# Convolution in VectorE's gaps between score levels, three modulation tiles summed in its place, out projection ahead of the ones products

## What is computed

```python
# modulation, for both layers: 24 tiles of 512 columns (tiles 0 to 11 layer 0, 12 to 23 layer 1)
mod[l] = silu(c) @ mod_w[l] + mod_b[l]            # 1024 -> 6 * 1024
# layer 0
q, f_raw, i_val, g_out, z, xbc, dt_raw = split(h @ w_in)
o_a = hgrn2_chunk_scan(q, 1 - f, i_val, log(f))    # gated recurrence, 8 heads of 128
o_a = group_rms_norm(o_a, hg_norm, 8) * silu(g_out)
xbc = silu(causal_dwconv(xbc, conv_w, conv_b))     # 4 taps, 1536 channels = 12 blocks of 128
xs, bm, cm = split(xbc)
y = ssd_chunk_scan(xs, dt, a, bm, cm) + d_skip * xs    # 16 heads of 64
o_b = group_rms_norm(y * silu(z), ssm_norm, 2)     # two groups of 512
x = x + gate * (concat(o_a, o_b) @ w_out)          # 2048 -> 1024
```

## Time and profile before

| | us |
|---|---|
| three executions | 1159.43, 1163.57, 1165.64 (median 1163.57) |
| profiled execution | 1162.93 |
| its span, first to last instruction | 1161.2 |
| PE busy | 1105.4 (95% of the span) |
| DVE busy | 428.9 (37%) |
| ACT busy | 266.7 (23%) |
| mean granted clock of TensorE | 0.974 of full |

### The profile page before, as it was taken

One profiled execution on the slowest core, in us unless ns is written; L12 is line 12 of the kernel. 1 busy time (PEld: TensorE's weight loads), 2 busy tenths in 40 slices (PEclk: granted clock), 3 DMA queues, 4 the chain that ended last, 5 costly groups with the idle time before them and its releaser, 6 DMA issues.

```text
span 1161.2 us, 15296 instructions
## 1 busy us (share of the span) xinstructions
PE 1105.4 (95%) x6223; PEld 719.1 (62%) x6223; DVE 428.9 (37%) x951; ACT 266.7 (23%) x439; POOL 107.4 (9%) x138
## 2 busy tenths in 40 slices
PE   4899999998989999999999989999998999999997
PEld 2686688896358864444444568848887844444444
DVE  0353674247460131222111386874523411111213
ACT  2212111223340131111111255323321311111113
POOL 5012112020000010000000201311000100000000
PEclk9899899999989989999999999999988999999998
DMA  9797747247978459997999920100059599999992
GB/s 350 267 371 290 263 172 279 84 145 259 390 293 342 164 197 422 421 421 287 421 420 420 344 104 21 53 0 3 2 199 420 210 401 420 421 420 420 421 421 85
DMA packets 86452, 320.55 MB, mean 276 GB/s; under 512 B 9877, under 2 KB 11253, under 8 KB 61813
## 3 DMA queue, kind: packets, MB, share of 16 engines
q1 hardware_dynamic: 83144, 309.49, 68.2%
q0 software_dynamic: 2448, 8.91, 2.0%
q10 hardware_dynamic: 796, 1.23, 0.3%
HBM read 316.47 MB, written 3.15 MB: 275 GB/s over the span
## 4 chain that ended last, share of the span: by engine, by line
PE 83%; SPq 6%; DMA 4%; DVE 3%; ACT 2%; issue 1%; ACTq 1%; DVEq 0%
PE bank L1178 17%; PE bank L811 17%; PE bank L1211 9%; PE bank L872 7%; PE bank L1103 6%; PE bank L822 5%; SPq L585 3%; PE bank L938 2%; DMA arena<-in_moe_w 2%; PE bank L844 1%; PE bank L1186 1%; PE bank L781 1%; PE bank L1475 1%; SPq L513 1%; PE bank L1465 1%
## 5 line engine op out<-in xcount | busy, mean ns | idle before, releaser
L811 PE MATMUL bank<-arena,ring 128*128 128x256 f32 x960 | 212.9, 383 | 3.9 <-ACT arena L1648 2.7
L811 PEld LDWEIGHTS bank<-arena,ring 128*128 128x128 f32 x960 | 183.3, 192 | 30.2 <-issue 3.9
L1178 PE MATMUL bank<-ring,arena 128*64 128x512 f32 x704 | 153.7, 592 | 0.0
L1178 PEld LDWEIGHTS bank<-ring,arena 128*64 128x64 f32 x704 | 50.4, 137 | 99.4 <-issue 99.4
L2386 DVE TENSOR_TENSOR arena<-arena,bank 128x512 f32<-128x512 f32 x17 | 18.1, 1068 | 224.5 <-PE bank L1178 224.5
L872 PE MATMUL bank<-arena,ring 128*128 128x256 f32 x384 | 86.0, 388 | 2.8 <-issue 2.8
L1178 PE MATMUL bank<-arena 128*64 128x512 f32 x384 | 84.4, 593 | 2.1 <-DMA arena<-in_moe_w 2.1
L1103 PE MATMUL bank<-arena 128*128 128x256 f32 x336 | 84.3, 398 | 2.0 <-DVE arena L2404 2.0
L872 PEld LDWEIGHTS bank<-arena,ring 128*128 128x128 f32 x384 | 74.8, 195 | 13.9 <-issue 3.2
L1103 PEld LDWEIGHTS bank<-arena 128*128 128x128 f32 x336 | 63.6, 199 | 11.5 <-issue 3.7
L1211 PE MATMUL bank<-ring,arena 128*64 128x512 f32 x288 | 63.8, 595 | 0.0
(11 more groups left out here) (373 smaller groups left out, 1360.6 us busy)
## 6 DMA issues: line engine op xcount, KB each, us to landing
ring<-in_moe_w SPq DMA_DIRECT2D x112, 1024.0 KB, 16.0
arena<-in_moe_w SPq DMA_DIRECT2D x80, 1024.0 KB, 19.0
ring<-in_mod_w SPq DMA_DIRECT2D x24, 2048.0 KB, 11.3
ring<-in_ev_w_in SPq DMA_DIRECT2D x13, 2048.0 KB, 12.8
ring<-in_od_w_rkv SPq DMA_DIRECT2D x6, 2048.0 KB, 13.3
ring<-in_ev_w_out SPq DMA_DIRECT2D x4, 2048.0 KB, 17.3
ring<-in_od_w_o SPq DMA_DIRECT2D x2, 2048.0 KB, 10.2
token_rows<-arena SPq DMA_DIRECT2D x2, 1024.0 KB
```

Source lines behind the costliest of these rows:

```text
L811: mm = pe.matmul(ps[:, c * S:(c + 1) * S], w_cols(slot)[:, k, (2 * half + c) * P:(2 * half + c + 1) * P], src[:, k, :], start=(k == 0), st ...
L1178: mm = pe.matmul(bank[4 + half][e * C:(e + 1) * C, :], hgT[:, kb, e * C:(e + 1) * C], piece(slots[e], kb), start=(kb == 0), stop=(kb == KB ...
```

## The change

Five edits, all in layer 0.

- `conv(b)` becomes a function, called in DVE's loop over the score levels: blocks 0 to 5 after `level_mult(5)`, 6 to 9 after `level_diff(7)` and the step of dt, 10 and 11 after `level_mult(7)`. ACT's silu of the convolution moves ahead of the evacuation of g_out.
- Modulation tiles 12, 13 and 14 are summed by DVE (`mod_sum`) where the convolution stood, into `buf(7)`; three products of ones (`ones_slide`, made by POOL) put them into strips 0, 1 and 2 of the row bank. Their slots come free by `mod_summed`.
- The modulation steps between the pairs of HGRN2 outputs are gone; the first one left, tile 15, follows the sum of squares. The transposes wait for `o_evac` one by one.
- `gate_scan` puts line 2206 and line 2243 together into DVE's decay loop at h = 3.
- The modulation columns move into PE's decay loop at h = 14 and their taking on DVE to h = 16; the out projection's first tile goes ahead of the ones products of y, which come before the second tile.

```diff
@@ -62,6 +62,7 @@
 MOD_DVE = 12
+MOD_LATE = 15
 NSUB = 4
@@ -359,7 +360,12 @@
             return [g for g, (a, b) in enumerate(MOD_GROUPS) if a <= m < b][0]
-        mod_acc = [buf(10)[:, i * W:(i + 1) * W] for i in (0, 1, 3, 2)]
+        ones_slide = buf(1)[:, 3 * W:3 * W + 63]
+        mod_acc_early = [buf(10)[:, i * W:(i + 1) * W] for i in (0, 1, 3, 2)]
+        mod_acc_late = [buf(7)[:, i * W:(i + 1) * W] for i in range(MOD_LATE - MOD_DVE)]
...
+        def mod_acc(m):
+            return mod_acc_early[m % 4] if m < MOD_DVE else mod_acc_late[m - MOD_DVE]
         def mod_slot(m):
@@ -529,7 +535,7 @@
                 at = places[l, kind].index(n)
-                if kind == "mod" and MOD_FIRST <= 12 * l_mod + j < MOD_DVE:
+                if kind == "mod" and MOD_FIRST <= 12 * l_mod + j < MOD_LATE:
                     sp.wait_ge(mod_summed, 12 * l_mod + j + 1 - MOD_FIRST)
@@ -711,7 +717,8 @@
             pool.wait_ge(proj_full, FULL_IN)
-            link(pool.memset(slide[1], 0.0))
+            link(pool.memset(buf(1)[:, 2 * W:3 * W + 63], 0.0))
+            pool.memset(ones_slide[:, 31:32], 1.0)
             pool.tensor_copy(slide[1][:, :, 31], csilu[:]).then_inc(basics, 1)
@@ -842,23 +849,21 @@
                         mm = pe.matmul(row_bank[32 * c:32 * (c + 1), :], slide[g][:, k, 31 - i:63 - i],
-                                       w_cols(slot)[:, k, :], start=(m == a and r == 0), stop=(m == b - 1 and r == 1),
+                                       w_cols(slot)[:, k, :], start=(r == 0 and (m == 0 or m == MOD_LATE and c == 3)), stop=(m == b - 1 and r == 1),
                                        skip_group_check=True)
...
                 for q in range(4):
-                    mm = pe.matmul(bank[6][:, 4 * m + q:4 * m + q + 1], mod_acc[m % 4][:, q * P:(q + 1) * P],
+                    mm = pe.matmul(bank[6][:, 4 * m + q:4 * m + q + 1], mod_acc(m)[:, q * P:(q + 1) * P],
                                    ones[:, 0:1], start=True, stop=True)
                 mm.then_inc(mod_full, 1)
-            mod_next = [MOD_DVE]
+            mod_next = [MOD_LATE]
             def modulation_step():
                 if mod_next[0] < 24:
-                    if mod_next[0] == 12:
-                        pe.wait_ge(basics, 3)
                     modulation(mod_next[0], bank[0])
@@ -983,7 +988,6 @@
                 mm.then_inc(o_full, 1)
-                modulation_step()
             pe.wait_ge(dt_ready, 1)
@@ -994,9 +998,10 @@
             pe.wait_ge(conv_silu, 1)
-            pe.wait_ge(o_evac, 4)
             for u in range(4):
                 tt, half = u // 2, u % 2
+                if u in (1, 2):
+                    pe.wait_ge(o_evac, u + 2)
                 if u == 3:
@@ -1004,6 +1009,13 @@
+            pe.wait_ge(basics, 3)
+            pe.wait_ge(mod_summed, MOD_LATE - MOD_FIRST)
+            for i in range(MOD_LATE - MOD_DVE):
+                mm = pe.matmul(bank[0][32 * i:32 * (i + 1), :], ones_slide[:, 31 - i:63 - i], mod_acc(MOD_DVE + i),
+                               start=True, stop=False, skip_group_check=True)
+            mm.then_inc(mod_full, MOD_LATE - MOD_DVE)
             pe.wait_ge(xdt_ready, 3)
@@ -1024,6 +1036,7 @@
                 mm.then_inc(stat_full, 1)
+            modulation_step()
             pe.wait_ge(cb_ready, 2)
@@ -1051,18 +1064,26 @@
                     head_out(h - 3)
-            mod_columns(1, bank[2])
...
-            pe.wait_ge(squares_ready, 1)
-            pe.wait_ge(dec_diff, NH)
-            for g in range(GROUPS):
-                for k in range(4):
-                    mm = pe.matmul(bank[4][:, g * S:(g + 1) * S], ones[:, 0:P], fT[:, 4 * g + k, :],
-                                   start=(k == 0), stop=(k == 3))
-            mm.then_inc(stat_full, 1)
-            pe.wait_ge(mod_taken, 3)
-            out_projection(0, places[0, "out"][0], 4, lambda i: oa[:, i, :] if i < KB else yT[:, i - KB, :],
-                           lambda j: pe.wait_ge(oa_ready, 1) if j == 0 else pe.wait_ge(ob_ready, 1))
+                if h == NH - 2:
+                    mod_columns(1, bank[2])
...
+            def out_ready(j):
...
+                if j == 0:
+                    pe.wait_ge(mod_taken, 3)
+                    pe.wait_ge(oa_ready, 1)
+                elif j == 1:
+                    pe.wait_ge(squares_ready, 1)
+                    pe.wait_ge(dec_diff, NH)
+                    for g in range(GROUPS):
+                        for k in range(4):
+                            mm = pe.matmul(bank[4][:, g * S:(g + 1) * S], ones[:, 0:P], fT[:, 4 * g + k, :],
+                                           start=(k == 0), stop=(k == 3))
+                    mm.then_inc(stat_full, 1)
+                else:
+                    pe.wait_ge(ob_ready, 1)
...
+            out_projection(0, places[0, "out"][0], 4, lambda i: oa[:, i, :] if i < KB else yT[:, i - KB, :], out_ready)
             def moe(l, k):
@@ -1738,6 +1759,8 @@
             level_exp(7)
+            act.wait_ge(conv_done, XBLK)
+            act.activation(xpad[:, :, TAPS - 1:], xpad[:, :, TAPS - 1:], ACT.Silu).then_inc(conv_silu, 1)
             act.wait_ge(mod_full, MOD_DVE)
@@ -1747,8 +1770,6 @@
                 act.activation(dst(fT), bank[6 + u % 2][:], ACT.Square).then_inc(o_evac, 1)
-            act.wait_ge(conv_done, XBLK)
-            act.activation(xpad[:, :, TAPS - 1:], xpad[:, :, TAPS - 1:], ACT.Silu).then_inc(conv_silu, 1)
             for u in range(4):
@@ -2015,9 +2036,10 @@
                 slot, count = mod_slot(m)
-                acc = mod_acc[m % 4]
+                acc = mod_acc(m)
                 dve.wait_ge(tile_landed[slot], 16 * count)
-                dve.wait_ge(mod_full, max(MOD_FIRST, m - 3))
+                if m < MOD_DVE:
+                    dve.wait_ge(mod_full, max(MOD_FIRST, m - 3))
                 link(ts_(acc, w_cols(slot)[:, 0, :], csilu[:, 0:1], None, ALU.mult))
@@ -2127,6 +2149,16 @@
                     ins.then_inc(score_evac, 1)
+            def conv(b):
...
+                dve.wait_ge(proj_evac, 18)
+                tmp = ctmp[:, b % 2, :]
+                wt = lambda j: col("ev_conv_w", j * XBLK + b)
+                link(ts_(tmp, xpad[:, b, 0:S], wt(0), col("ev_conv_b", b), ALU.mult, ALU.add))
+                for j in range(1, TAPS - 1):
+                    link(stt(tmp, xpad[:, b, j:j + S], wt(j), tmp, ALU.mult, ALU.add))
+                stt(xpad[:, b, TAPS - 1:], xpad[:, b, TAPS - 1:], wt(TAPS - 1), tmp, ALU.mult,
+                    ALU.add).then_inc(conv_done, 1)
             level_diff(0)
@@ -2143,6 +2175,12 @@
                     mod_sum(m)
+                if i == 5:
+                    for b in range(6):
+                        conv(b)
+                elif i == 7:
+                    for b in range(10, XBLK):
+                        conv(b)
                 if i < 7:
@@ -2152,6 +2190,8 @@
                     ts_(dts[:, 0, :], bank[7][0:NH, 0:S], dt_bias[:], None, ALU.add).then_inc(dtz, 1)
+                    for b in range(6, 10):
+                        conv(b)
                 if i == 6:
@@ -2171,15 +2211,8 @@
             gains(0, 1)
-            dve.wait_ge(proj_evac, 18)
-            for b in range(XBLK):
-                tmp = ctmp[:, b % 2, :]
-                wt = lambda j: col("ev_conv_w", j * XBLK + b)
-                link(ts_(tmp, xpad[:, b, 0:S], wt(0), col("ev_conv_b", b), ALU.mult, ALU.add))
-                for j in range(1, TAPS - 1):
-                    link(stt(tmp, xpad[:, b, j:j + S], wt(j), tmp, ALU.mult, ALU.add))
-                stt(xpad[:, b, TAPS - 1:], xpad[:, b, TAPS - 1:], wt(TAPS - 1), tmp, ALU.mult,
-                    ALU.add).then_inc(conv_done, 1)
+            for m in range(MOD_DVE, MOD_LATE):
+                mod_sum(m)
             dve.wait_ge(dtN_full, 1)
@@ -2200,15 +2233,18 @@
             dve.wait_ge(proj_evac, 26)
-            for u in range(4):
-                dve.wait_ge(stat_rstd, u + 1)
-                for h in (2 * u, 2 * u + 1):
-                    ins = stt(oa[:, h, :], oa[:, h, :], col("ev_hg_norm", h), fT[:, h, :], ALU.mult, ALU.mult)
-            count[0] += 1
-            ins.then_inc(dve_chain, 1)
-            normed = count[0]
...
...
+            def gate_scan():
...
+                for u in range(4):
+                    dve.wait_ge(stat_rstd, u + 1)
+                    for h in (2 * u, 2 * u + 1):
+                        ins = stt(oa[:, h, :], oa[:, h, :], col("ev_hg_norm", h), fT[:, h, :], ALU.mult, ALU.mult)
+                link(ins)
+                tt_(buf(2), buf(2), buf(10), ALU.mult).then_inc(oa_ready, 1)
...
...
+            dve.wait_ge(mod_full, MOD_LATE)
             def decay_diff(h):
@@ -2237,15 +2273,14 @@
                     decay_mult(h - 1)
-                if h == NH + 1:
...
-                    dve.wait_ge(dve_chain, normed)
-                    tt_(buf(2), buf(2), buf(10), ALU.mult).then_inc(oa_ready, 1)
+                if h == 3:
+                    gate_scan()
```

(5 more changed lines are left out.)

## The result

The changed kernel takes 1151.88 us, the median of five executions (1150.28 to 1155.23), against 1163.57 before: a ratio of 0.989, with 0.9865 to 0.9914 as its 95% interval. 1151.0 was forecast.

A forecast was written before the change was run, and what follows sets the result against it. PE, busy 95%, was taken as the bound, then DVE and the modulation loads. Out projection 15.6 us earlier less 3.8 for ones products gives 11.8, called 12: 1162.9 - 12 = 1151.0 us, range 1146 to 1157.

The forecast's parts named there:

- The convolution at no cost: Score levels: twelve blocks of 1.89 us fit DVE's idle gaps, the tight two with 1.0 and 0.8 us to spare.
- Three tiles summed by DVE: Ahead of the decay loop: PE sheds three 1.85 us steps, pays 0.9; first decay row moves from 293.99 to about 286.3.
- Tile 23 stops it: Decay loop: tile 23 cannot land before 310.8, so PE waits and only 5.2 of 8.6 us come through.
- The rate: Modulation loads after tile 17: 5.47 us per 2.10 MB tile, 384 GB/s, queue never empty from 269 on.
- Tail and out projection: End of decay loop: out projection begins at 328.5 instead of 344.14, 15.6 us earlier, paying back 3.8 for ones products.
- its first tile (a quarter of 55.42, 13.9 us): Out projection: the first tile takes 13.9 us and covers the last y, ACT's squares and their wait.
- The sum: Layer 0's mixer: 15.6 - 3.8 = 11.8 us gained, called 12 us and counted whole to the kernel's end.
- the second rival: PE's clock drops at waits for transfers and thin work until 328, costing 2.0 to 5 us: about 1154.5; chance 0.2.
- Rivals 3 and 4: Layer 0's experts' transfers absorb most gain, about 1161, chance 0.05; convolution overruns its gaps, about 1165, chance 0.04.
- the fourth rival: Score levels: blocks at 2.0 times their length overrun DVE's gaps, PE waits 14 us; about 1165, chance 0.04.

The follow-up runs named there:

- e9: Kernel before with only the convolution moved into DVE's gaps, ACT's silu ahead and transposes waiting one by one; median 1163.72 us, 0.999 of before.
- e10: Changed kernel plus four PE products nobody reads, in the wait before the first score level; median 1151.43 us, 0.9894 of before.
- e4: Changed kernel with modulation tiles 18 and 19 issued ahead of tile 17 on SP's queue; median 1147.8 us, 0.9842 of before.
- e5: Changed kernel plus six PE products nobody reads, three before the wait for tile 22, three before head 14; median 1152.62 us, 0.9887 of before.
- e1: Kernel before with only convolution in the gaps, three tiles summed by DVE, first modulation step after the sum of squares; median 1159.38 us, 0.9957 of before.
- e3: Changed kernel with the ones products of y back ahead of the out projection's first tile; median 1158.34 us, 0.9943 of before.
- e7: Changed kernel with ten convolution blocks instead of six in DVE's first gap, none in the second; median 1163.26 us, 0.9977 of before.
- e8: Changed kernel with the gate product back in the tail of DVE's decay loop; median 1155.82 us, 0.9919 of before.
- e2: Kernel before with only gate at h = 3, modulation columns at h = 14, out projection's first tile ahead of the ones products; median 1159.14 us, 0.9946 of before.
- e6: Changed kernel with tiles 18, 19 loaded ahead of 17, plus unread PE products: four before the first score level, three before head 14; 1144.22 us, 0.9826 of before.

## Why the prediction was right

The total was right, and most steps with it; one term was mis-sized, and gains outside the stage, partly luck, made up for most of it.

- **The convolution at no cost** held: both gaps had the 1.0 and 0.8 us to spare that were worked out, and ACT's silu began at 246.5, for about 248. e9 shows that the move alone pays only the silu's wait.
- **Three tiles summed by DVE** held: the first decay row moved by 24.37 - 16.12 = 8.25 us from the first output, where 293.99 to 286.3, 7.7, was forecast. The three ones products took 0.99 us from start to start, for an estimate of 0.9.
- **Tile 23 stops it** held: its step begins 41.1 us from the first output, forecast 310.8 - 269.6 = 41.2, and the waits stand at tiles 22 and 23 as said; the second was 0.42 us for 2 because the slow step of tile 22 used up the rest (e10, with that step at full clock, has 1.52 and 2.06). The reason given, SP's order with tile 17 blocked ahead, is what e4 shows.
- **The rate** was the measured one: 5.40 us for 2.10 MB are 389 GB/s, and the experts reach 421. The Trainium skill (DMA: Bandwidth & Descriptors, Where 436 GB/s comes from) has transfers from memory bound near 358 GB/s; this trace doesn't agree, and the measurement decides.
- **Tail and out projection**: it begins 59.5 us from the first output, forecast 328.5 - 269.6 = 58.9. The ones products inside took 3.62 for 3.8. The step that failed is the next one, "its first tile (a quarter of 55.42, 13.9 us)": it took 16.26. The sum had the 2.0 us of slow ones products (5.78 for 3.8) vanish with the new order. The low clock stayed where it was, about the last heads, and now lies on the first quarter instead, 2.2 us from one start to the next.
- **The sum** for the stage was 11.8. Measured are 9.3, and 11.8 in e5, where the clock holds. So **the second rival came true** in this execution, near the lower end of its price (2.0 to 5), but not quite as it was told. It set the falls at the waits for transfers and in the thin work until 328. All six kernels that have both waits for tiles and no remedy at them (after, e1, e3, e7, e8, e10) do show a granted clock of 0.50 behind one of the two. Behind tile 22 (after, e3, e7, e8) that cost next to nothing: row h = 8 comes 43.7 to 44.2 us from the first output, for a forecast of 313.5 - 269.6 = 43.9. Behind tile 23 (e1, e10) it comes at 45.1 to 45.3. What cost the changed kernel its 2.4 us is the other fall, at the last heads, and that one needs no new wait: e2 has no wait for a tile and shows it too. I gave the rival 0.2; but a fall at or behind the last heads came in eight of the nine kernels that have neither unread products nor the new load order in the stage (all but e10), the kernel before among them, where it stood in the ones products' 5.78 us. So a price for it belonged in the sum. The Trainium skill (TensorE: Matmul & The Clock Gate, Loop structure matters more than you think) warned of waits for transfers between products; at tiles 22 and 23 the trace agrees, at the last heads of e2 and at level 3 it doesn't explain the fall.
- **Why the total came out**: 9.3 from the stage, 1.25 from an earlier first output and 0.5 behind the stage are 11.05, for a forecast of 12. The 1.25 come from a fall of the clock at level 3 after (3.4 us) in place of one at level 0 before (4.9), less 0.3 by which level 0 began later after; that is luck of the two executions. That the medians differ by 11.7 as well was not taken apart.
- **Rivals 3 and 4**: layer 0's experts begin at 414.4 after and 424.9 before, 10.6 us earlier, and keep it; none of the gain is absorbed. e7 brought about the lateness that the fourth rival describes. The rival had the whole gain go with 14 us of wait; with 4.7 nearly all of it was gone (0.9977 of before), since the low clock behind the wait costs 5.4 us more. By that its threshold, a factor of 1.9 on the blocks, was too high. The row that it read as POOL alone (2.36 us at 239.05) has DVE at work beside it, on the scores from 239.46 and then until 242.1; what the 3.38 us row has beside it is DVE's product at 231.75.

What stays open: why the clock falls at one level or at the last heads in one execution and not in the next, with the same work, and whether unread products change the odds. With one profiled execution of each kernel no run here settles it.

## What to carry to other kernels

When a load is late, ask first whether its queue was idle before it: an in-order queue that is blocked at one load holds back every later one whose slot is free, and one blocked load put behind two others was worth 3.8 us here, with 2.9 more of clock in the profiled execution. Price a new wait of PE with the clock behind it, ask whether a later wait absorbs that, and give the thin work a price for the clock even where no wait is new. Before you credit a remedy with a clock that held, look whether it also held in a kernel without the remedy. An order that fills an idle engine may earn nothing alone; count it by what can then be put in its old place.

## What the runs showed of the hardware

- The clock fell on a PE that had not waited: 3.4 us lost at level 3 of the changed kernel, and in e2 a granted clock of 0.81 from 328 to 330 with PE busy throughout. Behind the 2.09 us of wait at level 0 before, a fall cost 4.9 us (23.12 from level 0's scores to level 1's, 18.19 after). Behind that same wait, there in ten of the kernels, level 0's scores took anything from 3.76 to 7.06 us.
- The same stage without an edit took 120.5, 118.7 and 118.9 us in three kernels, and the granted clock is what differs. A single pair of profiled executions can't tell a remedy for the clock from this.
- With four unread products in level 0's wait the clock held there in two kernels of two (e10, e6); without them it held in one of ten. In both a later level had the fall (6 and 1), as in the changed kernel (3).
- DVE's late level 5 (6.4 us late) makes PE wait 4.7 us in e7, and PE loses 10.2 us: 3.3 more in the scores and 2.1 in the tile behind, both at a granted clock of 0.50.
